# mLSTM cell: prompt chunk matmuls in three fp32r passes, key sums moved to POOL and ACT, head sums and gate strips moved

## The reference

```python
gates = q @ w_gates[:M_INNER] + k @ w_gates[M_INNER:2*M_INNER] + v @ w_gates[2*M_INNER:] + b_gates
i_pre, log_f = gates[..., :M_HEADS], log_sigmoid(gates[..., M_HEADS:])
# per chunk, per head; state C (512 x 512), n (512)
s   = (q @ k.T) * w_intra                       # t x j
num = s @ v + w_inter * (q @ C)
den = sum(s, axis=j) + w_inter * (q @ n)
h   = num / maximum(abs(den), exp(-m_t))
C   = decay * C + (k * wk).T @ v
n   = decay * n + sum_j(wk * k)
y   = ((sigmoid(o) * layernorm(h) * head_norm + skip * xc) * silu(z)) @ w_out
```

## Time and profile before

| | us |
|---|---|
| median of 3 runs | 2629.16 (2627.26 to 2630.09) |
| the profiled execution | 2625.33 |
| its span | 2623.6 |

### The profile page before, as it was taken

One profiled execution on the slowest core, in us unless ns is written; L12 is line 12 of the kernel. 1 busy time (PEld: TensorE's weight loads), 2 busy tenths in 40 slices (PEclk: granted clock), 3 DMA queues, 4 the chain that ended last, 5 costly groups with the idle time before them and its releaser, 6 DMA issues. The chain is left out here.

```text
span 2623.6 us, 34624 instructions
## 1 busy us (share of the span) xinstructions
PE 2364.7 (90%) x13407; PEld 1973.1 (75%) x13407; DVE 1044.9 (40%) x1912; ACT 676.7 (26%) x1188; POOL 144.3 (5%) x229
## 2 busy tenths in 40 slices
PE   5998877886998999999999999993999999999997
PEld 4997766773888988998899899872558557558557
DVE  3201136874115320242043123304773763672673
ACT  3224434552124331332132223311211210210210
POOL 0000000000000000000000000001210210210210
PEclk8999978995899999999999999995998998998999
DMA  6710111120341222222222322216664664564561
GB/s 190 101 49 24 33 37 46 34 72 28 91 134 42 74 99 101 67 74 109 76 75 73 117 75 83 84 70 191 177 193 116 177 193 117 162 200 124 175 194 68
DMA packets 315850, 271.77 MB, mean 104 GB/s; under 512 B 60986, under 2 KB 261658, under 8 KB 315615
## 3 DMA queue, kind: packets, MB, share of 16 engines
...
## 5 line engine op out<-in xcount | busy, mean ns | idle before, releaser
L368 DVE TENSOR_TENSOR sb_wlo<-sb_wraw,sb_whi 128x1024 fp32r<-128x1024 f32 x100 | 122.3, 1225 | 772.8 <-ACT sb_whi L363 769.8
L384 PE MATMUL ps<-sb_h1h,sb_whi 128*128 128x360 f32 x1152 | 255.7, 330 | 11.1 <-DVE sb_h1l L430 7.9
L384 PE MATMUL ps<-sb_h1h,sb_wlo 128*128 128x360 f32 x1152 | 254.1, 329 | 1.6 <-issue 1.6
L384 PE MATMUL ps<-sb_h1l,sb_whi 128*128 128x360 f32 x1152 | 253.9, 329 | 0.0
L384 PEld LDWEIGHTS ps<-sb_h1h,sb_whi 128*128 128x128 f32 x1152 | 200.3, 190 | 14.8 <-issue 10.6
L384 PEld LDWEIGHTS ps<-sb_h1h,sb_wlo 128*128 128x128 f32 x1152 | 201.2, 190 | 2.1 <-issue 2.1
L384 PEld LDWEIGHTS ps<-sb_h1l,sb_whi 128*128 128x128 f32 x1152 | 200.9, 190 | 0.0
L1503 PE MATMUL ps<-sb_vt,sb_kw 128*128 128x512 f32 (+1 forms) x288 | 158.0, 679 | 4.8 <-DVE sb_scs L1644 2.0
L1493 PE MATMUL pm<-sb_cst,sb_qs 128*128 128x512 f32 x256 | 135.5, 611 | 0.0
L363 ACT ACTIVATE sb_whi<-sb_wraw 128x1024 fp32r<-128x1024 f32 x100 | 106.0, 1061 | 113.9 <-PE ps L384 89.8
L384 PE MATMUL ps<-sb_hh,sb_whi 128*128 128x360 f32 x480 | 113.6, 345 | 8.5 <-DVE sb_hl L430 8.5
...
## 6 DMA issues: line engine op xcount, KB each, us to landing
...
```

Source lines behind the costliest of these rows:

```text
L368: dve.tensor_tensor(wlo[q][:, :], wraw[q][:, :], whi[q][:, :].bitcast(F32), ALU.subtract)\
L384: last = pe.matmul(ps[s][:, g, 0:GRP], w[:, kk, c * P:(c + 1) * P], x[:, kk, g * GRP:(g + 1) * GRP], start=(kk == 0 and i == 0), stop=(kk ...
```

## The change

1. The prompt chunks' matmuls with values on one side, scores·values and keys·values, are made in three fp32r passes instead of one float32 matmul. `kw`, `vt`, `swb` get high parts `kh`, `vh`, `swh` (by ACT) and low parts `kl`, `vl`, `swl` (by DVE). The scores·values product goes from the front of the chunk to behind the queries·state blocks.
2. The key sums leave PE. POOL multiplies keys by their weights (`weighted_keys`), loaded as a broadcast row `chw` from a new DRAM row `krow`; ACT sums them with `accum_out` (`key_sums`), DVE adds them to `nst` (`key_state`) at the end of the chunk.
3. In `put`, DVE keeps the multiplication; the addition (`gated`) and `put_low` go to POOL.
4. `chin` has two buffers of q, k, v; the gates get two buffers `chga` of their own. SP's order changes: chunk b + 3 ahead of the store of sample b, the gates behind the state load.
5. Head sums: `hn_pe` runs for g = 0, 1, 2 behind blocks 3, 4, 5 of the product.
6. Gate strips: `wg` is 8 columns wide, and the three matmuls go to partitions 0, 32 and 64 of `pm[0]`. The rows come out with 4 instructions for both gates, and the input gate rows are moved down by a DMA.

```diff
-    wg = sb("wg", [P, 12, 36], X0 + 2 * 4416)
+    wg = sb("wg", [P, 12, 2 * MH], X0 + 2 * 4416)
-    chin = [rbuf(f"chin{i}", [P, 5, 4, P]) for i in range(3)]
+    chin = [rbuf(f"chin{i}", [P, 3, 4, P]) for i in range(2)]
+    chga = [rbuf(f"chga{i}", [P, 2, 4, P]) for i in range(2)]
...
         for g in range(3):
-            r = 64 if g == 1 else 0
-            last = pe.matmul(pm[g // 2][r:r + 36, 0:GRP], wg[:, i, :], st[i % 3][:, 0, g * GRP:(g + 1) * GRP],
+            last = pe.matmul(pm[0][32 * g:32 * g + 2 * MH, 0:GRP], wg[:, i, :], st[i % 3][:, 0, g * GRP:(g + 1) * GRP],
                              start=False, stop=False, skip_group_check=True)
...
# gates_dve
-        for f, dst in ((0, gi), (1, fx)):
-            for g in range(2):
-                r = 64 * g + 32 * f
-                done(dve.tensor_scalar(dst[:, 1 + g * GRP:1 + (g + 1) * GRP], pm[0][r:r + MH, 0:GRP], brow[r:r + MH, 0:1],
-                                       None, ALU.add))
...
+        for g in range(3):
+            r = 32 * g
+            w = n if g == 2 else GRP
+            dve.tensor_scalar(fi[:, 1 + g * GRP:1 + g * GRP + w], pm[0][r:r + 2 * MH, 0:w], brow[r:r + 2 * MH, 0:1], None, ALU.add)
...
# cell_sp
-        chunk_load(sp, h, 3)
+        chunk_load(sp, h, 2)
+        chunk_weights(sp, h, 2)
+        chunk_gates(sp, h, 2)
         for b in range(DECB):
+            if b + 3 < NP:
+                chunk_load(sp, h, b + 3)
+                chunk_weights(sp, h, b + 3)
             sp.wait_ge(sem("c_done"), due(NU * h + u_samp(b, 3) + 1))
             sp.dma_start(state(o["sample_mlstm_c"], b), scs[b % 2][:, :, :]).then_inc(sem(f"sc_out{b % 2}"), 16)
-            if b + 4 < NP:
-                chunk_load(sp, h, b + 4)
             if b + 2 < DECB:
                 state_load(b + 2)
+            if b + 3 < NP:
+                chunk_gates(sp, h, b + 3)
...
# cell_gp, new
+        def gated(c):
+            wait_gates(gp, h, c)
+            gp.wait_ge(sem("u_mul"), NCH * h + c + 1)
+            gp.tensor_tensor(u[:, :, 0:n], u[:, :, 0:n], gb[:, :, 0:n], ALU.add).then_inc(sem("u_add"), 1)
+        def put_low(c):
+            gp.wait_ge(sem("uh_done"), NCH * h + c + 1)
+            gp.tensor_tensor(ul[:, :, cols], u[:, :, 0:n], uh[:, :, cols].bitcast(F32), ALU.subtract).then_inc(sem("ul_done"), 1)
+        def weighted_keys(c):
+            gp.tensor_tensor(kwt[:, :, 0:n], chin[c % 2][:, 1, :, 0:n],
+                             chw[c % 2][:, 0:n].rearrange("p (a t) -> p a t", a=1).to_broadcast([P, 4, n]), ALU.mult)\
+                .then_inc(sem("kwt_ready"), 1)
...
         for c in range(NP):
+            if c >= 1:
+                gated(c - 1)
             if c + 1 < NP:
                 exponents(c + 1)
+            weighted_keys(c)
+            if c >= 1:
+                put_low(c - 1)
+            if c + 1 < NP:
+                queries(c + 1)
             if c >= 1:
                 sequence_keys(c - 1)
-            if c + 1 < NP:
-                queries(c + 1)
...
# cell_pe
-            pe.matmul(pm[0][0:n, :], swb[r][0:n, 0:n], vt[r][0:n, :], start=True, stop=(c == 0))
             small(c + 1)
-            pe.matmul(SM[0:n, 0:1], swb[r][0:n, 0:n], ones[0:n, 0:1], start=True, stop=(c == 0))
             if c > 0:
...
                 for k in range(4):
-                    pe.matmul(pm[0][0:n, :], qs[r][:, k, 0:n], cst[:, k, :], start=False, stop=(k == 3))
+                    pe.matmul(pm[0][0:n, :], qs[r][:, k, 0:n], cst[:, k, :], start=(k == 0), stop=False)
...
-            for k in range(4):
-                last = pe.matmul(SM[:, 8 + k:9 + k], kw[r][0:n, k * P:(k + 1) * P], ones[0:n, 0:1], start=True, stop=True)
+            pe.matmul(SM[0:n, 0:1], swb[r][0:n, 0:n], ones[0:n, 0:1], start=(c == 0), stop=True)
+            wait_apart(pe, sem("sw_hi"), NP * h + c + 1)
+            wait_apart(pe, sem("sw_lo"), NP * h + c + 1)
+            wait_apart(pe, sem("kv_lo"), 2 * NP * h + 2 * c + 1)
+            for i, (w, v) in enumerate(((swh, vh), (swh, vl), (swl, vh))):
+                last = pe.matmul(pm[0][0:n, :], w[r][0:n, 0:n], v[r][0:n, :], start=(c == 0 and i == 0), stop=(i == 2))
             last.then_inc(sem("small_ready"), 1)
+            pe.wait_ge(sem("kv_lo"), due(2 * NP * h + 2 * c + 2))
             for k in range(4):
...
-                pe.matmul(U_[u % 2], kw[r][0:n, k * P:(k + 1) * P], vt[r][0:n, :], start=True, stop=True)\
-                    .then_inc(sem("u_ready"), 1)
+                for i, (w, v) in enumerate(((kh, vh), (kh, vl), (kl, vh))):
+                    last = pe.matmul(U_[u % 2], w[r][0:n, k * P:(k + 1) * P], v[r][0:n, :], start=(i == 0), stop=(i == 2))
+                last.then_inc(sem("u_ready"), 1)
...
# cell_act: score_high(c+1) behind turned(c+1), key_sums(c) ahead of norm(c)
+            for k in range(4):
+                last = act.activation(kwt[:, k, 0:ROWN[c]], kwt[:, k, 0:ROWN[c]], ACT.Copy, accum_out=nsum[c % 2][:, k:k + 1])
...
# cell_dve
             if c > 0:
                 put(c - 1)
+            score_low(c)
+            value_low(c)
             if c > 1:
                 sample_state(c - 2, 0)
                 sample_state(c - 2, 1)
-            if c > 0:
-                put_low(c - 1)
-                if c < 4:
-                    w_low(c - 1)
+            key_low(c)
             if c > 1:
                 sample_state(c - 2, 2)
                 sample_state(c - 2, 3)
+            if 0 < c < 4:
+                w_low(c - 1)
             small(c + 1)
...
             if c + 1 < NP:
                 scores(c + 1)
+            key_state(c)
...
# in_step of PE, layer 0; product calls mid(kk) after each block kk
-                    hn_pe(pe, m, 0)
-                    hn_pe(pe, m, 1)
-                    hn = lambda: hn_pe(pe, m, 2)
+                    hn = lambda kk: hn_pe(pe, m, kk - 3) if 3 <= kk < 6 else None
```

More of the change, by code:

```diff
@@ L309, in build @@
     ROWS = R0[0]
-    rown = [sb(f"row{i}", [P if i == 6 else MH, ICOL], ROWS + 4352 * i) for i in range(7)]
-    gi, lf, cb, mm_, msk, fx, rs = rown
+    rown = [sb(f"row{i}", [(MH, MH, MH, MH, MH, 2 * MH, P)[i], ICOL], ROWS + 4352 * i) for i in range(7)]
+    gi, lf, cb, mm_, msk, fi, rs = rown
+    fx = fi[0:MH, :]
     cst = rbuf("cst", [P, 4, MD])
@@ L340, in build @@
     x1T_d = scratch("x1T", [KT, P, TP])
+    krow_d = scratch("krow", [MH, ICOL])
     vnew_d = scratch("vnew", [DECB, DECT, 256])
@@ L386, in product @@
                                      start=(kk == 0 and i == 0), stop=(kk == k - 1 and i == 2))
-            if mid is not None and kk == k // 2:
-                mid()
+            if mid is not None:
+                mid(kk)
         last.then_inc(sem("ps_full"), 1)
@@ new lines, in chunk_load @@
+    def chunk_load(sp, h, c):
+        n = ROWN[c]
+        first = isinstance(h, int) and h == 0
+        if not first or c > 1:
+            wait_apart(sp, sem("kwt_ready"), NP * h + c - 1 if c > 1 else NP * h)
+            wait_apart(sp, sem("s_done"), NCH * h + c if c > 1 else NCH * h)
+            wait_apart(sp, sem("qs_ready"), NCH * h + c if c > 1 else NCH * h)
+        for i, src in enumerate((q_d, k_d, v_d)):
+            sp.dma_start(chin[c % 2][:, i, :, 0:n],
+                         src[bass.ds(4 * h, 4), :, COL0[c]:COL0[c] + n].rearrange("k p t -> p k t")).then_inc(sem(f"chin{c % 2}"), 16)
@@ new lines, in chunk_weights, with chunk_gates @@
+    def chunk_weights(sp, h, c):
+        n = ROWN[c]
+        sp.dma_start(chw[c % 2][:, 0:n], dram(krow_d, ICOL * h + 1 + COL0[c], [[0, P], [1, n]])).then_inc(sem(f"chw{c % 2}"), 16)
+    def chunk_gates(sp, h, c):
+        n = ROWN[c]
+        first = isinstance(h, int) and h == 0
+        if not first or c > 1:
+            wait_apart(sp, sem("u_add"), NCH * h + c - 1 if c > 1 else NCH * h)
+        for i, src in enumerate((ga_d, gb_d)):
+            sp.dma_start(chga[c % 2][:, i, :, 0:n],
+                         src[bass.ds(4 * h, 4), :, COL0[c]:COL0[c] + n].rearrange("k p t -> p k t")).then_inc(sem(f"chga{c % 2}"), 16)
@@ L1318, in cell_sp @@
         if not first:
-            chunk_load(sp, h, NCH - 1)
-        for c in range(3):
+            samp_load(sp, h)
+        for c in range(2):
             if not first:
                 chunk_load(sp, h, c)
+                chunk_weights(sp, h, c)
             if c == 0:
@@ L1325, in cell_sp @@
                 sp.dma_start(abc[:, :], dram(arow_d, ICOL * h + 1, [[0, P], [1, NPR]])).then_inc(sem("abc_in"), 16)
+            if not first:
+                chunk_gates(sp, h, c)
         state_load(0)
@@ L1416, in pre @@
                 pe.wait_ge(sem("k3_lo"), 2 * h + 2)
+            else:
+                pe.wait_ge(sem("kv_lo"), due(2 * NP * h + (0 if sample else 2 * c)))
             for i, bank in ((1, KT_), (2, VT_)):
@@ L1645, in sample_state, with key_low, value_low, score_low @@
                                      ALU.mult, ALU.add).then_inc(sem("c_done"), 1)
+        def key_low(c):
```

(25 more changed lines are left out.)

147 lines of the change are left out of this document (91 added, 56 removed).

## The result

| | before | after |
|---|---|---|
| median | 2628.21 (2626.07 to 2630.09, 4 runs) | 2545.09 (2537.44 to 2545.98, 4 runs) |
| the profiled execution, its span | 2625.33, 2623.6 | 2545.05, 2543.3 |

What follows compares the result with a forecast made beforehand. PE, busy 90% of the span, bounds the kernel; in the cell PE and DVE take turns. Head sums -35, strips -28.8, gate rows +1 and cell -20 make -83: 2546 us as a median, range 2518 to 2582.

Steps and rivals of the forecast that it cites:

- Head sums: First layer's projection: ten PE waits of 3.1 us go, -31.0, and two low-clock starts, -4; bounds -25 to -36.
- Gate strips: Gate groups in the q, k, v products: three strips run at once, 0.60 saved x 48 = -28.8; bounds 0 to -34.
- Rival B: Gate strips don't run three at a time because three writes go to one bank: item 0, 2575; chance 0.05.
- Gate rows: Copies of gate rows halve, about 2 us, against 2 to 3 more for `krow`: +1, between -2 and +4.
- PE's half of a chunk: Cell, chunks from 4 on: the part where PE sets the time falls from 7.83 to 6.86 us, -0.97.
- DVE's half: Cell, chunks from 4 on: the 6.54 us where DVE's chain sets the time lose L1757's place, 0.14.
- the cheaper state updates: DVE's half of a chunk: four state updates on PE take 0.70 each for 0.86, but this gives nothing.
- DVE is already full: Chunks 2 and 3: `w_low` (1.22) moves behind sample updates, DVE full to the end of PE's half; net +1.0 each.
- The hold by POOL: Cell: POOL's lock on DVE's two-input steps, `queries` perhaps over L1657: 0.1 us a chunk, between 0 and 1.1.
- The head's end: End of a head: PE waits for addition and low part, now on POOL: +1.5, and +0.5 for the sample block.
- A: The cell gives nothing, by POOL's lock on DVE's small steps or late DMAs: 2568, or 2580; chance 0.20.
- C: PE falls to the low clock inside the cell: +6.3 a chunk for 28 chunks, +176, so 2742; chance 0.05.

Runs made afterwards that it cites:

- two-strip run: Changed kernel with the third group of gate products back in the first one's strip, in the other bank: 2567.33 us, ratio 0.9762 to before.
- one-tensor form: Changed kernel with the denominator's two small two-tensor steps made tensor_scalar with one tensor and a per-partition scalar: 2535.44 us, ratio 0.9653 to before.

## Why the prediction was right, and where it was not

The time was right, and so were its three parts: 37.5 for 35, 26.5 for 27.8, 19.4 for 20. That the cell came out at 19.4 for 20 is in part luck: inside it larger errors cancelled. From the transposes in the traces before and after, over four heads and without chunk 0 of head 0: chunk 1 -2.6 us (forecast -4.4), chunks 2 and 3 -1.6 (+3.2), chunks 4 to 8 -21.6 (-20), the other chunks 0 -8.0 (-5.1, with the low parts in the shadow, though PE waits up to 0.9 us for one), the ends of the heads +15.7 (+8). Together -18.2 (-18.3).

- **Head sums.** As predicted. 17.03 - 13.66 = 3.37 us a product, ten times: the third sum's place in the stream costs the evacuation nothing, and the first scores are 37.6 us earlier, of which 3.9 lie beside the ten waits, the low-clock start among them.
- **Gate strips.** 7.45 - 6.83 = 0.62 us a group; 0.60 was forecast, and 0.57 was the estimate by the Trainium skill's 2.38 times ("TensorE: Matmul & The Clock Gate", Part 3). The two are too close for the row to tell them apart. Rival B, one bank, is out: three groups write one bank in 0.72 us, and the two-strip run has two banks and is the slower.
- **Gate rows.** +1 was forecast. In the changed kernel's trace the stage from the last convolution tail to the first keys is 2.7 us shorter, and from there to the first keys of chunk 0 it is 3.7 longer (20.75 for 17.08): +1.0, as forecast.
- **PE's half of a chunk** 6.89 us in head 0, forecast 6.86. The forecast was worked out from a loop head's chunk, and there it is 7.04: 0.2 short.
- **DVE's half** 6.08 us in a loop head (6.54 before), forecast 6.40; in head 0 5.91 (6.44 before). The step that failed is that of the cheaper state updates, "but there DVE's chain is the longer, and this gives nothing". The prediction took the 0.39 us from the end of `normed` to the transposes for a hand-over. But PE has no idle time in a steady chunk before, as its 106.55 of 107 us say; from its state updates on it goes from one block to the next, up to L1457 and L1438:

```profile
2098.43 4.03 PE L1503 MATMUL ps<-sb_vt,sb_kw 128*128 128x512 f32 x8
2102.30 1.04 PE L1420 MATMUL ps<-sb_ident,sb_chin 128*128 128x128 f32 x8
2103.17 1.06 PE L1426 MATMUL ps<-sb_chin 128*128 128x128 f32 x8
```

Where PE does wait for `normed`, it starts 0.10 us behind its end (the run without w_low, the line below, L1830 ending at 2040.44). So PE's own work set this half too. The passes took 0.63 us from the four state updates, and 0.21 came back as the wait for DVE's first one; with 0.15 in PE's half that is the 0.57 of a chunk. DVE's pair of 1.60 us in the run without passes is PE's pace seen from DVE. A steady chunk is 12.80 in head 0, 13.1 in the loop heads, and not 13.3.

```profile
2040.54 0.63 PE L1532 MATMUL pm<-sb_ident,sb_hb 128*128 128x128 f32 x4 [0.30 <-DVE sb_hb L1830]
```

- **w_low.** "DVE is already full" was the wrong reason. DVE waits 0.57 us for PE before its last sample update (the forecast said under 0.3; the trace before had 0.56, at 1901.39): these updates keep PE's pace, and the last one ends with PE's half. An instruction behind it is wholly on the path, however idle DVE was before: 1.22 us plus what it does to `queries`. Taking the low parts away changed nothing there; taking w_low away gave 4.5 us a head. The net of chunks 2 and 3, +1.0 each, was passed in two of the six chunks that it stood for, where the low clock came to it: chunk 3 of head 0 (16.05 for 14.55) and chunk 2 of head 2 (16.15 for 14.66). The other four are between -0.14 and +0.35, since the steady gain covers most of it.
- **The hold by POOL.** Forecast 0.1 us a chunk; nine of the 80 steps L1803 and L1804 took 0.67 to 1.23 us, 7.1 us more together than at 0.16 each, and the one-tensor form gave 9.9 of cell. In the steady chunks of head 0 of this trace nothing is held: in the one shown, `queries` waits 2.07 us for its DMA and starts when DVE is past these steps. It isn't always so. With the head's end on DVE, chunk 5 of head 0 has a step of 1.23 us and lasts 13.87. Here the Trainium skill's rule ("SBUF — State Buffer", "SBUF: two separate sides": two SBUF inputs, against a GpSimd instruction that reads SBUF) was the better guide than L1657 beside L1392, and its size was set by when the two meet. That a tensor_scalar with a per-partition scalar is free of it is what the rule implies, and none of the 80 steps of that run is held. But by the rule POOL's tensor_scalar (L1448), which reads SBUF too, would hold them as well, and here the rows decide: of 16 steps that began under it in the changed kernel, ten took 0.16 to 0.23 us and six 0.34 or 0.35.
- **The head's end.** +2.0 a head was forecast; giving it back was worth 2.7 in the cell, 3.2 by the medians. The forecast had the longer instructions, 1.26 us to the start of the output product, but not the low clock that goes with them in three heads of four.
- **DMA.** Two us of slack were enough but for one chunk: in chunk 7 of head 3 (13.36 us) PE's transposes wait for keys and values. The DMA engines are busy for 0.87 of the time over three steady chunks.

```profile
2445.04 1.09 PE L1514 MATMUL ps<-sb_ident,sb_chin 128*128 128x128 f32 x8 [0.34 <-DMA sb_chin<-scratch_v]
```

- **Rivals.** A happened in part and C in a few stretches; neither reached its point.

Whether w_low would be hidden on DVE ahead of the last sample update wasn't tried. Why the denominator's and the head end's gains overlap so much is open; the holds at the four ends of a head (0.85, 0.67 and 0.69 us beside the 1.23 above) are in both, 2.8 us of the 10.8 + 9.9 - 15.0 = 5.7.
